# Gated DeltaNet trunk on eight cores: chunk preparation split into two generators, three stages in one pipeline

## What is computed

```
ia = I + strict_lower(kb @ k.T * decay)
u  = solve(ia, v * beta)
w  = solve(ia, kb * exp(g))
qk = lower(q @ k.T * decay)
# then chunk by chunk, in order:
v_new = u_c - w_c @ S
o_c   = q_dec @ S + qk @ v_new
S     = S * exp(g_last) + k_dec.T @ v_new
```

## Time and profile before

| | us |
|---|---|
| runs | 4590.3 and 4594.4, median 4592.4 |
| the profiled execution | 4588.2 |
| its span, slowest core (2) | 4585.2 |
| spans of the 8 cores | 4570.1 to 4585.2 |
| mean granted TensorE clock | 0.695 to 0.704 of full speed |

### The profile page before, as it was taken

The page is one execution under the profiler, slowest core; times in us unless marked ns, Lnnn a source line. Parts: engine busy times, 40 slices in busy tenths (PEclk is TensorE's granted clock), DMA queues, the critical chain, the costliest instruction groups (busy, mean ns, idle before and its releaser), DMA issues.

```text
span 4585.2 us, 47992 instructions; the slowest of 8 cores (4570.1 to 4585.2 us)
## 1 busy us (share of the span) xinstructions
PE 2488.5 (54%) x13572; PEld 1372.0 (30%) x13572; DVE 2039.7 (44%) x4100; ACT 1480.8 (32%) x2571; POOL 733.0 (16%) x1064
## 2 busy tenths in 40 slices
PE   1245555555555455555555555554455465777769
PEld 1013233223223233322332233331233122333324
DVE  2135564555555455545555555552555022222212
ACT  3234433433443343344334432334233122111101
POOL 2011111111111111011111111100110121232313
PEclk9566666765666566667666656666666777898979
DMA  3010000000000000010000000000000411222231
GB/s 82 4 12 3 5 1 8 5 3 5 5 5 1 7 5 3 1 10 3 3 8 3 5 1 5 1 1 7 8 1 1 115 15 14 28 28 28 29 55 74
DMA packets 156399, 68.51 MB, mean 15 GB/s; under 512 B 145392, under 2 KB 145392, under 8 KB 156144
## 3 DMA queue, kind: packets, MB, share of 16 engines
q0 software_dynamic: 121744, 37.82, 7.8%
q1 hardware_dynamic: 34400, 27.62, 2.2%
HBM read 94.86 MB, written 8.39 MB: 23 GB/s over the span
## 4 chain that ended last, share of the span: by engine, by line
PE 40%; DVE 22%; ACT 15%; issue 12%; DMA 5%; POOL 3%; DVEq 1%; another core or an unknown queue 1%; ACTq 0%; SPq 0%; POOLq 0%
PE psum L239 24%; PE psum L322 10%; DVE UTw L254 8%; DVE xstream L254 5%; PE psum L370 5%; ACT L245 3%; DVE g_ndL L254 2%; DVE g_ndU L254 2%; DVE g_Msb L251 2%; DMA sc_w<-sc_w_in 2%; ACT g_kdec L248 1%; ACT g_kbg L248 1%; ACT g_craw L245 1%; ACT wn L245 1%; POOL xstream L258 1%
## 5 line engine op out<-in xcount | busy, mean ns | idle before, releaser
L245 ACT ACT_TABLE_LOAD x286 | 366.9, 1283 | 686.7 <-PE psum L239 335.5
L254 DVE SCALAR_TENSOR_TENSOR UTw<-psum,UTw 128x512 bf16<-128x512 f32 x768 | 499.1, 685 | 200.3 <-PE psum L239 193.2
L322 PE MATMUL psum<-hT,sc_w 128*128 128x512 bf16 x2048 | 474.5, 396 | 129.2 <-DMA sc_w<-sc_w_in 129.2
L239 PE MATMUL psum<-UTw,g_A 128*128 128x128 bf16 x1536 | 243.8, 262 | 366.8 <-DVE UTw L254 366.8
L251 DVE TENSOR_TENSOR g_Msb<-psum,maskB 128x256 bf16<-128x256 f32 x896 | 355.7, 419 | 169.1 <-PE psum L239 165.9
L239 PE MATMUL psum<-g_Msb,UTw 128*128 128x128 bf16 x1536 | 301.8, 268 | 232.9 <-DVE g_Msb L251 218.1
L239 PE MATMUL psum<-hT,g_w 128*128 128x512 bf16 x1024 | 372.8, 531 | 95.0 <-DMA g_w<-gdn_w_in 47.2
L254 DVE SCALAR_TENSOR_TENSOR xstream<-g_craw,gcw,xstream 128x512 f32<-128x512 f32 x384 | 300.9, 784 | 266.2 <-POOL xstream L258 236.6
L322 PEld LDWEIGHTS psum<-hT,sc_w 128*128 128x128 bf16 x2048 | 206.2, 101 | 397.0 <-issue 176.5
L258 POOL TENSOR_SCALAR xstream<-g_craw,gcw 128x512 f32<-128x512 f32 x128 | 88.4, 691 | 1382.8 <-ACT g_craw L245 1199.2
L370 PE MATMUL psum<-hT,yT 128*128 128x512 bf16 x1024 | 230.3, 388 | 95.5 <-DMA hT<-gdn_w_out 34.5
(11 more groups left out here) (142 smaller groups left out, 4258.9 us busy)
## 6 DMA issues: line engine op xcount, KB each, us to landing
sc_w<-sc_w_in POOLq DMA_DIRECT2D x64, 256.0 KB, 5.7
xstream<-x SPq DMA_DIRECT2D x16, 512.0 KB, 4.2
g_w<-gdn_w_in POOLq DMA_DIRECT2D x32, 256.0 KB, 4.3
xs<-x SPq DMA_DIRECT2D x16, 512.0 KB, 19.3
out<-xs SPq DMA_DIRECT2D x16, 512.0 KB, 2.7
g_wz<-gdn_w_in POOLq DMA_DIRECT2D x16, 256.0 KB, 4.8
hT<-gdn_w_out POOLq DMA_DIRECT2D x4, 1024.0 KB, 15.1
hT<-sc_w_out POOLq DMA_DIRECT2D x4, 1024.0 KB, 8.3
```

Of the source, the lines that this page charges most:

```text
L239: return P.add("pe", lambda e: e.matmul(out, lhsT=lhsT, rhs=rhs, start=start, stop=stop), reads, writes)
L245: return P.add("act", lambda e: e.activation(out=out, in_=in_, func=func, **kw), reads, writes)
L254: return P.add("dve", lambda e: e.scalar_tensor_tensor(out=out, in0=in0, scalar=scalar, in1=in1, op0=op0, op1=op1), reads, writes)
L322: P.add("pe", lambda e, wa=wa, kc=kc, c0=c0, b=bk[ty]: e.matmul(pbank(b), lhsT=wa[:, kc, :], rhs=hT[:, kc, c0:c0 + 512], start=(kc == 0), ...
```

## The change

`prep2` is cut into `pre(cp)`, its first three stages, and `inv(cp)`, the seven levels and u and w. The buffers between the two (g_A, g_kbg, g_vb) are doubled. g_sq and g_rn, scratch of the projection, move into the two hn buffers of the norm. Half 1's M moves from bank 2 to the second half of bank 3, and the u and w products from banks 2 and 3 to banks 4 and 7.

`pipeline` (three generators) takes the place of `drive_bg`. A round issues two stages of the tail of cp, one stage of the inverse of cp+1, one stage of the preparation of cp+2 if the tail is done, and one background step if banks 0 and 1 are free. The tail has 12 stages, so the preparation is issued in rounds 6, 7 and 8 of 16.

```
@@ -482,8 +482,9 @@
             o_oa = (xh(1, 1), ("xsA1", 1))
             o_qa = (wn[:, 0:512], "wn")
             o_ra = (wn[:, 512:1024], "wn")
-            sq = Rot("g_sq", [sb(f"g_sq{i}", [128, 512]) for i in range(1)])
-            rn = Rot("g_rn", [sb(f"g_rn{i}", [128, 512]) for i in range(1)])
+            sq = Rot("hn", [hn[0][:].bitcast(F32)])
+            rn = Rot("hn", [hn[1][:].bitcast(F32)])
+            rn.next = lambda: (hn[1][:].bitcast(F32), ("hn", 1))
             qT = sb("g_qT", [128, T], BF16)
             kT = sb("g_kT", [128, T], BF16)
             vT = [sb(f"g_vT{i}", [128, T], BF16) for i in range(2)]
@@ -494,10 +495,10 @@
             ndL = f4("g_ndL")
             ndU = f4("g_ndU")
             grow = f4("g_grow")
-            Abuf = b4("g_A")
+            Abuf = Rot("g_A", [b4(f"g_A{i}") for i in range(2)])
             Msb = b4("g_Msb")
-            kbg = b4("g_kbg")
-            vb = b4("g_vb")
+            kbg = Rot("g_kbg", [b4(f"g_kbg{i}") for i in range(2)])
+            vb = Rot("g_vb", [b4(f"g_vb{i}") for i in range(2)])
             qkmT = Rot("g_qkmT", [b4(f"g_qkmT{i}") for i in range(2)])
             qdT = Rot("g_qdT", [b4(f"g_qdT{i}") for i in range(2)])
             kdec = Rot("g_kdec", [b4(f"g_kdec{i}") for i in range(2)])
@@ -606,10 +607,11 @@
                 P.add("pool", lambda e: e.memset(S[:], 0.0), writes=[("g_S", 0), ("g_S", 1)])
                 P.add("pool", lambda e: e.memset(Sbf[:], 0.0), writes=["g_Sbf"])
                 st_ = {}
+                pst = {}
                 if DBG_STAGE < 2:
                     continue
 
-                def prep2(cp):
+                def pre(cp):
                     insts = [(cb, hh) for cb in range(2) for hh in range(2)]
                     live01[0] += 1
                     for cb in range(2):
@@ -644,37 +646,46 @@
                     qk_a, qk_r = qkmT.next()
                     qd_a, qd_r = qdT.next()
                     kd_a, kd_r = kdec.next()
+                    A_a, A_r = Abuf.next()
+                    kb_a, kb_r = kbg.next()
+                    vb_a, vb_r = vb.next()
                     for i, (cb, hh) in enumerate(insts):
                         c, h = 2 * cp + cb, hs[hh]
                         cs = slice(c * 128, (c + 1) * 128)
-                        STT(Abuf[:, i, :], psum[:, 0, cb * 256:cb * 256 + 128], beta[:, c, h:h + 1], ndL[:, i, :],
-                            ALU.mult, ALU.mult, PS(0) + ["g_beta", ("g_ndL", i)], [("g_A", i)])
+                        STT(A_a[:, i, :], psum[:, 0, cb * 256:cb * 256 + 128], beta[:, c, h:h + 1], ndL[:, i, :],
+                            ALU.mult, ALU.mult, PS(0) + ["g_beta", ("g_ndL", i)], [(A_r, i)])
                         TT("dve", qk_a[:, i, :], psum[:, 0, cb * 256 + 128:cb * 256 + 256], ndU[:, i, :], ALU.mult,
                            PS(0) + [("g_ndU", i)], [(qk_r, i)])
                         TT("pool", qd_a[:, i, :], qA[:, cs], grow[:, i, :], ALU.mult,
                            [qN + (c // 4,), ("g_grow", i)], [(qd_r, i)])
-                        AMUL(kbg[:, i, :], pT1[:, cb * 128:(cb + 1) * 128], bgam[:, c, h:h + 1],
-                             PS(1) + ["g_bgam"], [("g_kbg", i)])
+                        AMUL(kb_a[:, i, :], pT1[:, cb * 128:(cb + 1) * 128], bgam[:, c, h:h + 1],
+                             PS(1) + ["g_bgam"], [(kb_r, i)])
                         AMUL(kd_a[:, i, :], pT1[:, cb * 128:(cb + 1) * 128], kd[:, c, h:h + 1],
                              PS(1) + ["g_kd"], [(kd_r, i)])
-                        AMUL(vb[:, i, :], pT1[:, 256 + i * 128:256 + (i + 1) * 128], beta[:, c, h:h + 1],
-                             PS(1) + ["g_beta"], [("g_vb", i)])
+                        AMUL(vb_a[:, i, :], pT1[:, 256 + i * 128:256 + (i + 1) * 128], beta[:, c, h:h + 1],
+                             PS(1) + ["g_beta"], [(vb_r, i)])
                     live01[0] -= 1
-                    yield
+                    pst[cp] = dict(qk=(qk_a, qk_r), qd=(qd_a, qd_r), kd=(kd_a, kd_r), A=(A_a, A_r),
+                                   kb=(kb_a, kb_r), vb=(vb_a, vb_r))
+
+                def inv(cp):
+                    d0 = pst.pop(cp)
+                    (qk_a, qk_r), (qd_a, qd_r), (kd_a, kd_r) = d0["qk"], d0["qd"], d0["kd"]
+                    (A_a, A_r), (kb_a, kb_r), (vb_a, vb_r) = d0["A"], d0["kb"], d0["vb"]
                     cur, curr = UT0, [["UT0"], ["UT0"]]
                     p4 = [psum[:, 4, :].rearrange("p (a b c) -> p a b c", a=2, b=2),
                           psum[:, 7, :].rearrange("p (a b c) -> p a b c", a=2, b=2)]
-                    mbank = (3, 2)
+                    mbank = (3, 3)
                     pbk = (4, 7)
                     for lv in range(7):
                         for half in range(2):
                             for k in range(2):
                                 i = 2 * half + k
-                                MM(psum[:, mbank[half], k * 128:(k + 1) * 128], Abuf[:, i, :], cur[:, i, 0, :],
-                                   [("g_A", i)] + curr[half], PS(mbank[half]))
+                                MM(psum[:, 3, i * 128:(i + 1) * 128], A_a[:, i, :], cur[:, i, 0, :],
+                                   [(A_r, i)] + curr[half], PS(mbank[half]))
                         yield
                         for half in range(2):
-                            TT("dve", Msb[:, 2 * half:2 * half + 2, :], v3(psum[:, mbank[half], 0:256]),
+                            TT("dve", Msb[:, 2 * half:2 * half + 2, :], v3(psum[:, 3, 256 * half:256 * half + 256]),
                                maskB[:, lv, 2 * half:2 * half + 2, :], ALU.mult,
                                PS(mbank[half]) + [("maskB", lv)], [("g_Msb", half)])
                             for k in range(2):
@@ -696,14 +707,14 @@
                         cur, curr = nxt, nxtr
                     curr = curr[0] + curr[1]
                     for i in range(NI):
-                        MM(psum[:, 2, i * 128:(i + 1) * 128], cur[:, i, 0, :], vb[:, i, :], curr + [("g_vb", i)], PS(2))
+                        MM(psum[:, 4, i * 128:(i + 1) * 128], cur[:, i, 0, :], vb_a[:, i, :], curr + [(vb_r, i)], PS(4))
                     for i in range(NI):
-                        MM(psum[:, 3, i * 128:(i + 1) * 128], kbg[:, i, :], cur[:, i, 0, :], curr + [("g_kbg", i)], PS(3))
+                        MM(psum[:, 7, i * 128:(i + 1) * 128], kb_a[:, i, :], cur[:, i, 0, :], curr + [(kb_r, i)], PS(7))
                     yield
                     u_a, u_r = u_sb.next()
                     w_a, w_r = wT_sb.next()
-                    ACTF(u_a[:], v3(pbank(2)), AF.Copy, PS(2), [u_r])
-                    ACTF(w_a[:], v3(pbank(3)), AF.Copy, PS(3), [w_r])
+                    ACTF(u_a[:], v3(pbank(4)), AF.Copy, PS(4), [u_r])
+                    ACTF(w_a[:], v3(pbank(7)), AF.Copy, PS(7), [w_r])
                     st_[cp] = dict(u=(u_a, u_r), w=(w_a, w_r), qk=(qk_a, qk_r), qd=(qd_a, qd_r), kd=(kd_a, kd_r))
 
                 def recur(c):
@@ -766,12 +777,32 @@
                     yield from recur(2 * cp + 1)
 
                 ncp = DBG_NCHUNK // 2
-                drive_bg([prep2(0)], bg)
+
+                def step(g):
+                    if g[0] is None:
+                        return
+                    try:
+                        next(g[0])
+                    except StopIteration:
+                        g[0] = None
+
+                def pipeline(ga, gb, gc):
+                    A, B, C = [ga], [gb], [gc]
+                    n = 0
+                    while A[0] is not None or B[0] is not None or C[0] is not None:
+                        step(B)
+                        step(B)
+                        step(A)
+                        if B[0] is None:
+                            step(C)
+                        n += 1
+                        if bg[0] is not None and live01[0] == 0:
+                            step(bg)
+
+                drive([pre(0)])
+                pipeline(inv(0), None, pre(1) if ncp > 1 else None)
                 for cp in range(ncp):
-                    gens = [tail(cp)]
-                    if cp + 1 < ncp:
-                        gens.insert(0, prep2(cp + 1))
-                    drive_bg(gens, bg)
+                    pipeline(inv(cp + 1) if cp + 1 < ncp else None, tail(cp), pre(cp + 2) if cp + 2 < ncp else None)
                 if bg[0] is not None:
                     drive([bg[0]])
                 elif p + 1 < DBG_NPAIRS and not overlap_ok(p + 1):
```

## The result

The changed kernel takes 4921.8 us in the median of 11 runs, the kernel before 4594.8 in 10. The ratio is 1.0724, with a 95% interval of 1.0667 to 1.078: slower by 7.2%. The forecast was 4900 us (+6.7%).

A forecast was written before the change was run, and what follows sets the result against it. The prediction took a latency loop between TensorE and VectorE, not a full engine, as the bound. Eight head pairs at +38.9 us add 311 us to the profiled 4588.2 us: 4900 us (+6.7%), range 4690 to 5050.

The forecast's parts named there:

- level 0: First inverse level: g_UTw queued behind the second S update on VectorE, ending 9.9 us after u products start.
- level 1: Second inverse level: g_Msb products wait behind gate and norm products on TensorE; ends 16.8 us after u products start.
- level 2: Third inverse level: output operation waits for ScalarE, costing about 1 us as before; ends 21.9 us after u products start.
- level 3: Fourth inverse level: the whole preparation stands in it, 11.3 us in place of 2.6; ends 33.2 us after u products start.
- levels 4 to 6: Last inverse levels, sharing bank 3: half 0's g_Msb waits for all four M products, 3.06 us each in place of 2.6.
- last step of a pair: A head pair's last inverse, with no preparation beside it: 34.3 us, 3.3 less than before.
- pair start: At a head pair's start, the second chunk pair's preparation stands in the first inverse: 12.8 us more.
- pair without background: Head pair without the next pair's projection beside it: 12.8 + 6 x 4.9 - 3.3 = +38.9 us.
- background step: One of 49 steps of the next head pair's projection: price kept at 2.0 us each, so nothing added.
- rival A: Preparation hides in VectorE's waits: a step takes 34.3 us, 4434 us in all, faster by 3.4%; chance 0.07.
- rival C: Background steps bunch in the inverse-only rounds, all at 3.07 us: 5212 us in all; chance 0.09.
- Rival B: Preparation's products keep TensorE's clock high: a step takes 38.6 us, 4676 us in all, within 2%; chance 0.11.

The follow-up runs named there:

- e3: Changed kernel with a round's order tail, inverse, tail in place of tail, tail, inverse: ratio 1.0506 to the kernel before.
- e5: Changed kernel with the preparation cut finely, at most two of its sixteen VectorE operations between inverse stages: 4501.4 us, ratio 0.9713 to the kernel before.
- e1: Kernel before with only both halves' M products put in bank 3: ratio 1.0192 to the kernel before.
- e2: Changed kernel with half 1's M back in bank 2 except in the level where the preparation holds it: quickest run 4839.8 us, no interval.
- e12: Changed kernel with finely cut preparation, round order tail, inverse, tail, and half 1's M in bank 2 where no preparation holds it: profiled execution 4327.8 us.
- e7: Changed kernel with finely cut preparation, inverse first in each round, half 1's M in bank 2 in four levels: 4352.0 us, ratio 0.9426 to the kernel before.
- e6: Changed kernel with the inverse first in each round, two tail stages in rounds 1 to 4, then one, preparation whole: ratio 1.0147 to the kernel before.
- e11: Kernel before with only g_sq and g_rn moved into the two hn buffers: ratio 1.0003 to the kernel before.
- e10: Kernel before with a background step after every third stage in place of every second: 4389.5 us, ratio 0.9552 to the kernel before.
- e8: Changed kernel with background steps only in rounds 1, 2, 3, 5, 14, 15 and 16: ratio 1.0356 to the kernel before.
- e9: Changed kernel with background steps only in rounds 9 to 15: ratio 1.0668 to the kernel before.

## Why the prediction was right

Level by level, from T:

| | predicted | measured |
|---|---|---|
| level 0 ends | 9.9 | 9.5 |
| level 1 | 16.8 | 16.0 |
| level 2 | 21.9 | 21.3 |
| level 3 | 33.2 | 33.0 |
| levels 4 to 6, each | 3.06 | 3.17 |
| next u products | 42.5 | 42.5 |
| last step of a pair | 34.3 | 33.9 to 34.5 |
| pair start | +12.8 | +13.2 |
| pair without background | +38.9 | +40.2 to 41.1 |
| background step | 2.0 | 2.04 |

Level 0. The g_UTw pair does stand behind the second g_S (3114.97, 3115.69), and moving it ahead of that (e3) took back the 1.3 us.

Level 1. The g_Msb products wait behind gate and norm products, as worked out; level 2's wait for the output operation is there with 2.26 us.

Level 3. The preparation stands whole in the inverse, and it is the largest term: 8.6 us of the step beyond a plain level. Cutting it finely (e5) took 4.9 us of the step back. What the prediction had not priced is how little the same sixteen operations cost when spread: rival A was wrong for this kernel, but most of the 6.7 us of VectorE work do fit into VectorE's idle time if they stand two at a time. What stays in e5 is mostly the wait for the preparation's products.

Levels 4 to 6. The coupling through one bank is right (e1, e2), the term was too small by 0.11. From the g_UTw pair's end to g_Msb it takes 0.62 us (its idle time in e1's rows, as in the changed kernel) in place of my 0.52, from there to g_UTw 1.26 (2935.22 to 2936.48) in place of 1.13, and that pair 1.29 in place of 1.41. The 1.13 came from the earlier trace rows, where each g_Msb waits for TensorE. Now the second waits for the first's semaphore and the pair lasts 0.95, which stood in the order rows of the change and which I did not price. Put into the kernel before, the bank costs 1.7 us a step and not seven times 0.52, because the disturbed levels absorb it.

A pair. 40.2 to 41.1 against 38.9: the six inner steps make +29.9 on core 3 and +30.7 on core 6 in place of 6 x 4.9 = 29.4, the pair start is 0.4 more (62.9 less 49.7 us, from the last g_u of a pair to the next one's first), and the last step gains 2.9 and not 3.3.

The background. The price was right, 2.04, but for a reason that the prediction left open. It said that the rounds cover either sort and so add nothing. They don't cover alike: the earlier trace rows's two prices, 1.45 and 3.07, were no bounds but two mixtures, and the mean moves from 1.36 (e12) to 2.16 (e2). Place and number do part of that. The loop around does another: e5 and e7 issue in the same rounds at 1.41 and 1.99, and e2 in those of the changed kernel at 2.16. Here the shift of 11 to 13 steps a chunk pair happened to leave it. The sign that the prediction named for rival C, a background step over 75 us, did show (79.16 us); the pair as a whole says that C didn't hold, since the other chunk pairs were cheaper (62.43). The sign was a bad one.

Rival B falls for this kernel. The step's granted clock is 0.62, where it was 0.64, the gate products take 3.62 us as before, and the eight passes 2.02. The next step has a granted clock of 0.54 and lasts 42.72 us where its neighbour lasts 42.58, so the step's length hardly follows the clock. But what B described, the preparation's products at the high level, came about in e6 and e7, where it is worth about 0.9 us of a step; so the clock is a small part of what the order gains there. The scratch buffers cost nothing (e11), as forecast. Not tried was the changed kernel without any preparation, so that its whole price rests on the level's length and on e5.

In sum: 8 x 38.9 = 311 us were forecast, and 309.2 measured between first and last g_u. That agrees better than its parts do. A pair of core 6 gives 7 x 41.1 + (41.1 - 13.2) = 316 even without a dearer background, since the first pair's start lies outside. On the other hand three of five pairs with background took 413.1 to 415.4 us before, on the same core 2, and not the 409.8 that I worked from, which takes some 13 us off the difference. So what was forecast too small (a pair by 1.3 to 2.2 us) and what was counted too large offset each other, and the agreement of the sum is partly luck.'s pair without background was read 1.5 us too short as well; that moves the old price from 2.01 to 1.98 and nothing else.

## What to carry to other kernels

On in-order queues, interleaving generators is a choice of positions: here the pipeline hid a stage only where its instructions stood in pieces that fit the waits of the loop, and the stage laid whole into the latency loop cost its whole length. Before such a change, write down for one period what stands between each pair of dependent instructions on the engine that both wait for. How often, and so where, a background generator is fed in is a parameter worth trying first; here one number gave 4.5%.

## What the runs showed of the hardware that I had not expected

- Two g_Msb operations on one PSUM bank, the second waiting for the first's semaphore, last 0.95 us together, in e1 as in the changed kernel, where each operation alone is 0.42 (e2's rows). A pair without that wait lasts 0.75 in e7 and e12. How much of the 0.52 us a level is this, and how much half 0's waiting for half 1's products, the runs don't separate.
- A background step of the same instructions costs 1.4 or 2.0 us, while the pair without background stays at 311.2 to 312.9 (the kernel before and e10) or 352.7 to 353.9 us (the changed kernel, e8 and e9). Where in the rounds the difference of 0.6 us arises, in which queue, the runs don't settle.
- The eight g_GR passes take 2.02 us at a granted clock of 0.50 in the changed kernel and 1.11 at 1.00 in e6, with the same products in another order. On TensorE the gate products had ended 7.8 us before them in the changed kernel (3120.90, 3128.73), and 4.5 us before them in e6 (2979.92, 2984.45). Whether that is the reason wasn't tried.
